# Tokens behind the first experts only normalised, their scale and bias moved to the column pieces and to GpSimd, and TensorE's overflow branch placed ahead of the ending

## The reference

```python
mod = silu(c) @ ada_w[i] + ada_b[i]
sh1, sc1, g1, sh2, sc2, g2 = split(mod, 6)
h = x * (1 + sc1) + sh1
y = mixer_i(h)                               # neighbourhood, then grouped-query
x = layer_norm(alpha * x + (1 + g1) * y, ln_g[i, 0], ln_b[i, 0])
h = x * (1 + sc2) + sh2
y = hierarchical_moe(h)                      # 32 experts, 2 per token
x = layer_norm(alpha * x + (1 + g2) * y, ln_g[i, 1], ln_b[i, 1])

def layer_norm(x, g, b):
    mu, var = x.mean(-1), square(x - mu).mean(-1)
    return (x - mu) * rsqrt(var + 1e-5) * g + b
```

## Time and profile before

| | |
|---|---|
| median of three runs | 1537.4 us (1534.27 to 1539.09) |
| the profiled execution's own time | 1536.41 us |
| its span, from first to last instruction | 1534.6 us |
| mean granted TensorE clock | 0.957 of full speed |
| busy: PE, DVE, ACT, POOL | 1365.2, 547.1, 213.0, 85.5 us |
| read from HBM | 530.27 MB |

### The profile page before, as it was taken

The page is one execution under the profiler, slowest core; times in us unless marked ns, Lnnn a source line. Parts: engine busy times, 40 slices in busy tenths (PEclk is TensorE's granted clock), DMA queues, the critical chain, the costliest instruction groups (busy, mean ns, idle before and its releaser), DMA issues.

```text
span 1534.6 us, 28498 instructions
## 1 busy us (share of the span) xinstructions
PE 1365.2 (89%) x12850; PEld 869.8 (57%) x12850; DVE 547.1 (36%) x1251; ACT 213.0 (14%) x570; POOL 85.5 (6%) x91
## 2 busy tenths in 40 slices
PE   7999999999999998879879787888999798798794
PEld 4886488578886655436436343467655364354451
DVE  3596659665843221111111105584211111111113
ACT  2230123022332000000000002442100000000000
POOL 3100111000003000000000001100200000000000
PEclk9999999999999999989889899999999998998998
DMA  9657945878869999999999997338999999999995
GB/s 345 224 195 260 334 170 201 284 269 300 316 269 397 413 427 427 426 426 427 427 427 425 428 398 276 110 112 339 398 416 427 426 427 426 427 426 427 426 421 200
DMA packets 95001, 533.31 MB, mean 348 GB/s; under 512 B 5121, under 2 KB 7361, under 8 KB 71057
## 3 DMA queue, kind: packets, MB, share of 16 engines
q1 hardware_dynamic: 91264, 519.40, 83.8%
q0 software_dynamic: 3600, 11.94, 2.2%
HBM read 530.27 MB, written 1.05 MB: 346 GB/s over the span
## 4 chain that ended last, share of the span: by engine, by line
PE 61%; DMA 29%; DVE 7%; ACT 1%; issue 1%; DVEq 0%; SPq 0%; ACTq 0%
PE bk L453 26%; PE bk L913 16%; DMA AR<-in_moe_w_down 14%; DMA ring<-in_moe_w_down 14%; PE bk L945 8%; PE bk L976 4%; DVE mpart L1061 3%; PE bk L449 2%; PE bk L672 1%; ACT AR L1890 1%; DVE AR L1053 1%; PE bk L687 1%; PE bk L643 1%; DMA ring<-in_w_in 1%; DVE sm L1064 1%
## 5 line engine op out<-in xcount | busy, mean ns | idle before, releaser
L913 PE MATMUL bk<-ring,AR 128*32 128x128 f32 x4480 | 268.2, 409 | 1.8 <-DMA ring<-in_moe_w_up 1.8
L913 PE MATMUL bk<-AR 128*32 128x128 f32 x3712 | 223.1, 409 | 4.2 <-DMA AR<-in_moe_w_up 4.1
L1053 DVE TENSOR_TENSOR AR<-bk,AR 128x128 f32<-128x128 f32 (+2 forms) x106 | 41.3, 389 | 515.2 <-ACT AR L1890 449.7
L913 PEld LDWEIGHTS bk<-ring,AR 128*32 128x32 f32 x4480 | 176.7, 127 | 83.8 <-DMA ring<-in_moe_w_up 4.8
L453 PE MATMUL bk<-ring,AR 128*128 128x256 f32 (+2 forms) x736 | 213.5, 448 | 6.7 <-ACT AR L1890 3.4
L1890 ACT ACTIVATE AR<-bk 128x512 f32<-128x512 f32 (+4 forms) x174 | 70.4, 427 | 921.3 <-PE bk L913 757.3
L913 PEld LDWEIGHTS bk<-AR 128*32 128x32 f32 x3712 | 145.3, 127 | 74.1 <-DMA AR<-in_moe_w_up 7.1
L453 PEld LDWEIGHTS bk<-ring,AR 128*128 128x128 f32 x736 | 140.5, 194 | 71.8 <-issue 55.0
L945 PE MATMUL bk<-ring,AR 128*32 128x512 f32 x544 | 139.2, 711 | 43.9 <-DMA ring<-in_moe_w_down 43.9
L453 PE MATMUL bk<-AR,ring 128*128 128x256 f32 (+1 forms) x832 | 170.6, 364 | 1.6 <-DVE diag L1053 1.6
L453 PEld LDWEIGHTS bk<-AR,ring 128*128 128x128 f32 x832 | 147.4, 190 | 21.4 <-issue 3.5
(11 more groups left out here) (159 smaller groups left out, 876.6 us busy)
## 6 DMA issues: line engine op xcount, KB each, us to landing
ring<-in_moe_w_gate SPq DMA_DIRECT2D x36, 2048.0 KB, 29.0
ring<-in_moe_w_up SPq DMA_DIRECT2D x34, 2048.0 KB, 26.6
AR<-in_moe_w_up SPq DMA_DIRECT2D x30, 2048.0 KB, 29.9
ring<-in_moe_w_down SPq DMA_DIRECT2D x30, 2048.0 KB, 34.4
AR<-in_moe_w_gate SPq DMA_DIRECT2D x28, 2048.0 KB, 26.9
AR<-in_moe_w_down SPq DMA_DIRECT2D x26, 2048.0 KB, 34.3
ring<-in_ada_w SPq DMA_DIRECT2D x24, 2048.0 KB, 10.5
ring<-in_w_in SPq DMA_DIRECT2D x12, 2048.0 KB, 14.7
```

What stands on the lines that cost most here:

```text
L913: ins = eng.matmul(o[32 * f:32 * f + 32, 128 * m:128 * m + 128], XG[u][:, c, 32 * j:32 * j + 32], w[:, c, f::4], start=c == 0, stop=c == N ...
L1053: return eng.tensor_tensor(o, a, b, op)
```

## The change

Behind the first experts VectorE only subtracts the mean and multiplies by the deviation, one tensor_scalar for each tile, and tells "xn" at once. The gain and bias of that layer norm are combined with `mod` (`norm_columns(1, 1, 0, "comb1", 1)`, three small VectorE instructions in the first quarter of the first experts) and are applied when the transposed columns are written: ScalarE writes columns 0 to 3 of each tile, VectorE columns 4 to 7. For the residual GpSimd multiplies `X` by `ln_g` and adds `ln_b`, four tensor_tensor of 128x1024 behind its last rsqrt of the grouped-query layer; the two rows go to `RES`, in the arena, by loads behind "xn" in place of those of `norm_after(0)`. `out_quarter` waits for "res", and SyncE waits for it ahead of all weights of the second experts. The gate rows are made behind "r00". TensorE's test for overflow stands ahead of `down_rows` in both layers, with the ending in both arms.

```diff
+        RES = view(6912, D), view(7936, D)
@@ TensorE, grouped()
-                common(1, "g")
                 for t in range(NT):
                     norm_cols(1, t)
                 for f in ("k0", "k1", "q00", "K0", "K1", "q10", "r00"):
                     unit(f)
+                common(1, "g")
@@ TensorE, experts(i), last quarter
+                    def ending():
                         o = down_rows()
                         down_end(o, 0)
                         combine(0)
                         down_end(o, 1)
+                        combine(1)
+                    pe.wait_ge(sem("cnt"), i + 1)
+                    kept = pe.n, dict(pe.past), pe.last, list(n_results)
+                    with eng.If(eng.value_load(cnt[0:1, NE:NE + 1]) > CAP):
+                        ending()
+                        overflow(i)
+                    pe.n, pe.past, pe.last, n_results[:] = kept
+                    with eng.Else():
+                        ending()
@@ TensorE, behind experts(i)
-                pe.wait_ge(sem("cnt"), i + 1)
-                with eng.If(eng.value_load(cnt[0:1, NE:NE + 1]) > CAP):
-                    overflow(i)
@@ VectorE
-            def last_cols():
-                v.wait_ge(*filled("nT", 1, 1, 1))
+            def odd_cols(t):
+                v.wait_ge(*filled("nT", 1, t, 1))
                 for a in range(4):
                     c = 4 + a
-                    ins = ts(HT[:, c, 128:256], bank("nT", 1, 1, 1)[:, 128 * a:128 * a + 128],
-                             mod[:, 1, 8 + c:9 + c], ALU.mult, mod[:, 1, c:c + 1], ALU.add)
+                    ins = ts(HT[:, c, 128 * t:128 * t + 128], bank("nT", 1, t, 1)[:, 128 * a:128 * a + 128],
+                             COMB[:, 1, 0, c:c + 1], ALU.mult, COMB[:, 1, 1, c:c + 1], ALU.add)
@@ VectorE, out_quarter
+                if i:
+                    v.wait_ge(sem("res"), t + 1)
@@ VectorE, grouped()
-                last_cols()
+                odd_cols(0)
+                odd_cols(1)
@@ VectorE, experts(i), q == 0
+                            if not i:
+                                norm_columns(1, 1, 0, "comb1", 1)
@@ VectorE, last_norm(i)
+                if not i:
+                    for t in range(NT):
+                        v.wait_ge(sem("lrs"), n_dev[0] - 1 + t)
+                        v.tell(ts(X[:, t, :], X[:, t, :], bn_a[:, t, 0:1], ALU.subtract, st2[:, t:t + 1], ALU.mult), sem("xn"), 3 + t)
+                    return
@@ ScalarE, early_cols(t)
-                s.wait_ge(sem("mod"), 8)
-                for h in range(1 if t else 2):
+                s.wait_ge(sem("comb1"), 1)
+                s.wait_ge(*filled("nT", 1, t, 0))
+                for c in range(4):
+                    ins = act(HT[:, c, 128 * t:128 * t + 128], bank("nT", 1, t, 0)[:, 128 * c:128 * c + 128], ACT.Identity,
+                              bias=COMB[:, 1, 1, c:c + 1], scale=COMB[:, 1, 0, c:c + 1])
@@ ScalarE, grouped()
-                gate_rows(1, "g1", GB_)
                 for f in ("k0", "k1", "q00", "K0", "K1", "q10", "r00"):
                     take(f)
+                gate_rows(1, "g1", GB_)
@@ GpSimd
-            norm_after(0)
+            g.wait_ge(sem("xn"), 4)
+            for n, name in enumerate(("ln_g", "ln_b")):
+                small(RES[n], A[name][0, 1:2, :].to_broadcast([P, D]), "row1")
             for n, f in enumerate(ROPED):
                 ...
+            g.wait_ge(sem("row1"), 32)
+            for t in range(NT):
+                for h in range(2):
+                    g.wait_ge(*filled("nT", 1, t, h))
+                g.step(tt(X[:, t, :], X[:, t, :], RES[0], ALU.mult))
+                g.chain()
+                g.tell(tt(X[:, t, :], X[:, t, :], RES[1], ALU.add), sem("res"), t + 1)
@@ SyncE, ahead of the weights of experts(i)
+                if i:
+                    sp.wait_ge(sem("res"), 2)
```

More of the change, by code:

```diff
@@ L977, in combine @@
                                            start=True, stop=True), "cb", i, q, n, t)
-                    if q == NQ - 1:
+                    if q < NQ - 1:
+                        down(0)
+                        down(1)
+                        combine(0)
+                        combine(1)
+                        continue
+                    def ending():
                         o = down_rows()
@@ L1440, in deviation, with norm_columns @@
                 v.tell(ts(st[:, 28 + t:29 + t], bn_a[:, t, 1:2], LN_EPS, ALU.add), sem("lvar"), n_dev[0])
-            def last_cols():
-                v.wait_ge(*filled("nT", 1, 1, 1))
+            def odd_cols(t):
+                v.wait_ge(*filled("nT", 1, t, 1))
                 for a in range(4):
                     c = 4 + a
-                    ins = ts(HT[:, c, 128:256], bank("nT", 1, 1, 1)[:, 128 * a:128 * a + 128],
-                             mod[:, 1, 8 + c:9 + c], ALU.mult, mod[:, 1, c:c + 1], ALU.add)
+                    ins = ts(HT[:, c, 128 * t:128 * t + 128], bank("nT", 1, t, 1)[:, 128 * a:128 * a + 128],
+                             COMB[:, 1, 0, c:c + 1], ALU.mult, COMB[:, 1, 1, c:c + 1], ALU.add)
                     if a == 3:
-                        free(ins, "nT", 1, 1, 1)
+                        free(ins, "nT", 1, t, 1)
                     else:
                         v.step(ins)
-            def norm_columns(n, i, k):
+            def norm_columns(n, i, k, told, value):
                 sc, sh = mod[:, i, 8 * (k + 1):8 * (k + 1) + 8], mod[:, i, 8 * k:8 * k + 8]
@@ L1459, in norm_columns @@
                 v.chain()
-                v.tell(tt(COMB[:, n, 1], COMB[:, n, 1], sh, ALU.add), sem("comb"), i + 1)
+                v.tell(tt(COMB[:, n, 1], COMB[:, n, 1], sh, ALU.add), sem(told), value)
             def router_weights(i):
@@ L1533, in side @@
                     elif kind == "n":
-                        norm_columns(2 * i, i, 3)
+                        norm_columns(2 * i, i, 3, "comb", i + 1)
                     elif kind == "o":
@@ L1565, in neighbourhood @@
                 extract(6)
-                norm_columns(0, 0, 3)
+                norm_columns(0, 0, 3, "comb", 1)
                 gate_rows(0)
@@ L1869, in last_norm @@
                     ins = stt(X[:, t, :], X[:, t, :], st2[:, t:t + 1], LN_OUT[1], ALU.mult, ALU.add)
[L1870 to L1873, removed]
+                    v.tell(ins, sem("xl"), t + 1)
             for l in range(DEPTH):
@@ L2043, in early_cols @@
             def early_cols(t):
-                s.wait_ge(sem("mod"), 8)
-                for h in range(1 if t else 2):
[L2046 to L2054, removed]
+                s.wait_ge(sem("comb1"), 1)
[3 more added lines that the diff above has]
+                              bias=COMB[:, 1, 1, c:c + 1], scale=COMB[:, 1, 0, c:c + 1])
+                    if c == 3:
+                        free(ins, "nT", 1, t, 0)
+                    else:
+                        s.step(ins)
             def raw_cols(i, t):
```

## The result

The changed kernel is slower by 0.3%, at the edge of what can be told from no change: median of eight runs 1541.9 us (1537.47 to 1544.32) against 1537.3 us of eight of the kernel before (1534.27 to 1539.4), a ratio of 1.0029 [1.0017, 1.0040]. The profiled execution took 1537.47 us, the fastest of its eight, with a span of 1535.7; its granted clock was 0.954.

A forecast was written before the change was run, and what follows sets the result against it. It took the experts as bound by DMA and the grouped-query layer by its own chain, mostly VectorE. Terms -2.9 - 3.2 + 0.4 + 8.4 - 0.7 = +2.0 us on the median 1537.4 gave 1539.4 us, range 1531 to 1544.

The forecast's parts named there:

- The loads: First experts without the gain and bias loads: gate and up pieces end 1.3 us sooner, last down pieces land 2.7 sooner.
- The branch in the first experts: TensorE's overflow test ahead of the down rows costs 4.94 us, partly hidden; the stretch to the end piece gives -2.9 us.
- Rival (c): The branch costs more than 4.94 us ahead of the down rows: 1544.7 us if 8, 1549 if 10; chance 0.15.
- Statistics to "k0": Grouped-query layer's start: one tensor_scalar per tile, columns split over two engines, nothing in front of the transposes; -3.2 us.
- The gate rows: Behind "r00", their 1.85 us partly fill TensorE's 1.49 us wait for ScalarE; +0.4 us.
- GpSimd's four: Residual products and sums in the grouped-query layer each hold one two-input VectorE instruction about 2.1 us; +8.4 us.
- The end: Second experts with the branch ahead of the down rows: end piece done at 1515.6 us against 1516.3; -0.7 us.

The follow-up runs named there:

- g5: g1 with the two 0.52 MB gain and bias rows loaded again at their old places in the first experts, unread; 1536.5 us, ratio 0.9991.
- h2: g1 measured again, beside h3; 1533.6 us, ratio 0.9967 to the kernel before.
- e3: The changed kernel with only TensorE's overflow test put back behind the last combine; 1540.2 us, ratio 1.0020 to the kernel before.
- g1: The changed kernel with the residual on VectorE and TensorE's overflow test back behind the last combine (e2 and e3 together); 1534.4 us, ratio 0.9975.
- g3: g1 with a second, short test and branch ahead of the down rows that jumps over one instruction; 1533.1 us, ratio 0.9969.
- e2: The changed kernel with the residual's four products and sums moved from GpSimd to VectorE; 1532.1 us, ratio 0.9964 to the kernel before.
- h3: e2 measured again, beside h2; 1533.0 us, ratio 0.9972 to the kernel before.
- g2: e2 with the gate rows back in front of the transposes; 1532.0 us, ratio 0.9955 to the kernel before.

## Why the prediction was right and where it was not

The time lay in the range and the change within 0.3%, for the most part for the reasons given. By its steps:

1. **The loads**: right. -1.3 to the last hidden transpose was forecast; it is -1.2 and -1.1. The two profiles with these loads have 427.8 and 427.9 us there (before, g5), ten of the eleven without them 426.2 to 427.1, and one, h2, 428.3. The last down pieces' 2.7 us show in g5 as 2.6 from the start to the first combine.
2. **The branch in the first experts**: this is the term that was mis-sized. The step says "the branch costs 4.94, taken from the gap", and draws the first row at 907.6 - 902.7 behind the transpose. It takes 6.4 to 6.6 us in all fourteen places where it stands ahead, in both expert stages of seven profiles. What was wrong is that the price was read from the gap. "Same code, same full DMA queue" held: the jump itself takes 6.05 to 6.38 us ahead of the down rows and 6.15 to 6.30 behind the first experts' last combine (before, e3, g1, h2, g3, g5). But the gap of 4.94 leaves out the 1.43 us that ran under the last combine's matmuls. The prediction took the 4.94 as all that the profile shows of the branch; asked for the branch's own line, it has a record of 6.20 us, and from that some 6.4 could have been forecast. The first row itself took the 3.5 us forecast (3.64), the two behind it 4.46 in place of 3.8. From the first experts' start to the first combine both profiles of the changed kernel are 0.8 us better than before (442.7 against 443.6), not 2.9. Rival (c) had the direction, but its break-even of 7.9 us wasn't reached: against before the stretch still gains a little. That gain is the loads', not the branch's: with the loads gone and the branch behind, the first combine comes 1.5 to 2.1 us sooner still (e3, g1, h2).
3. **Statistics to "k0"**: right. VectorE's tensor_scalar takes 0.81 us (0.8 estimated; two in 1.69), and 10.98 us became 7.43 and 7.42: -3.6 where -3.2 was forecast. Of that some 0.9 comes from the branch's leaving: with it behind, the same distance is 8.3 to 8.4 us (g1, h2, g3, g5, e3). The other 2.6 are the 1.85 us of gate rows, which no longer stand between, and the 1.38 that TensorE waited for ScalarE, less what its transposes take longer (3.5 to 3.7 us against 2.88).
4. **The gate rows**: +0.4 forecast. "k0" to the first scores is 31.4 us in the changed kernel, +0.9, but 30.4 and 30.5 in e2 and h3 with the same order. So between 0 and +0.4, and the rest is the clock: the 48 matmuls from "k0" on take 21.83 us at a granted clock of 0.95 in the changed kernel, against 20.84 at 1.00 before and in e2.
5. **GpSimd's four**: right, in mechanism, place and size. +8.4 forecast; VectorE's three groups grew by 8.3, TensorE's wait by 8.31 (11.12 - 2.81), e2 took 8.7 off the median, and TensorE's way from the first scores to the second experts is 112.2 to 115.1 us in the three profiles that have them there, and 104.9 to 108.0 in the eight that don't (before, e2, h3, g1, h2, g2, g3, g5). In that long stretch part of it is the granted clock, 0.92 or 0.90 in those three and 0.89 to 0.95 in the eight: beside e2, also at 0.92, the first profile's 112.2 is 5.5 us more and not 6.6. By the exclusion that the Trainium skill states (SBUF — State Buffer, "Who interferes with whom") the full length of 9.6 us would be lost; the trace has 2.0 to 2.1 us lost by each of GpSimd's, which took 2.55 us in the mean, since the held instruction's own 0.4 to 0.75 us are no loss. So a held instruction lasts 2.45 to 2.82 us, and the rule describes it well. For rsqrt the prediction looked at VectorE alone. VectorE was indeed not held: its tensor_scalar of 128x1024 ran in 0.81 us beside the second rsqrt, as long as the one behind it. But GpSimd's own instruction grew, from 0.56 us to 0.91 in all twelve profiles with the tensor_scalar, and to 1.41 beside the scalar_tensor_tensor of 1.28 us in the kernel before. That fits GpSimd as the one that waited; which of the two gives way, no run here varies. SyncE's wait for "res" moved the first load of the second experts to 1001.61 us, as soon as GpSimd was through, at no cost that the last stage shows (461.0 against 461.2).
6. **The end**: missed by the same term as step 2. -0.7 was forecast; from the last hidden transpose to the last stage's first combine it is 15.7 us and, again, 16.3, against 15.6: +0.1 and +0.7. With 6.5 us for the branch the step's own working gives +0.3: the rows then end at 1515.5, behind the 1514.5 at which the end piece lands, so 1.0 of the 1.6 counts.

With 6.5 us for the branch step 2 is 1.6 us dearer and step 6 1.0, and the sum is +2.0 + 2.6 = +4.6 in place of +2.0; the two measurements have +4.6 and +3.2. That the first agrees to the tenth is luck, since the two measurements differ by 1.4 us.

What the change contains is worth keeping: with the residual on VectorE it is 0.28 to 0.45% faster than the kernel before (e2, h3, g2), and so faster than both kernels.

## What to carry to other kernels

Work moved to an idle engine is free only if what it touches is free too: look at what the busy engine is doing at that moment, not at its own share. A wide elementwise instruction on GpSimd held one of VectorE's two-input ones for nearly its whole length, while the same work on VectorE took half as long and fitted a gap. And see which side grew: beside tiny rsqrt it was GpSimd's instruction and not VectorE's. Price a jump by its own record and not by the gap that it leaves: a gap is what remains when the work that the engine still had in hand is over, and at another place less may be in hand. A test whose jump is short costs almost nothing (0.24 us).

## What was unexpected of the hardware

The far jump of TensorE took 6.05 to 6.38 us in twenty places (fourteen ahead of the down rows, six behind the first experts' last combine), with the DMA engines full each time (share 1.01 to 1.05), and 3.36 to 3.62 us behind the second experts' last combine, where they are idle (share 0.02, six places). Windows over the jump alone, of the changed kernel and then of the kernel before, with the columns of the earlier trace rows:

```profile
901.24:907.38 6.14, 0.00 (x0) 0.00 (x0) 0.05 (x1) 0.00 (x0) 0.00 (x0) 0.59 1.02 388
```

```profile
924.85:931.05 6.20, 1.43 (x4) 0.36 (x2) 5.28 (x10) 0.00 (x0) 1.95 (x2) 1.00 1.04 385
1522.11:1525.65 3.54, 1.60 (x4) 0.38 (x2) 2.57 (x4) 0.00 (x0) 0.00 (x0) 1.00 0.02 5
```

The DMA queues of the changed kernel from 901 to 907.5 us, and in e3 from 923.6 to 929 us (packets, MB, share):

```profile
q1 hardware_dynamic: 849, 2.45, 98.4%
q14 instruction: 4, 0.03, 1.4%
q8 instruction: 1, 0.02, 1.1%
```

```profile
q1 hardware_dynamic: 1033, 2.08, 103.8%
q8 instruction: 1, 0.02, 1.3%
```

The weights' packets are larger in the first (2.9 KB in the mean against 2.0), and packets of q14 lie in it (the same queue has five from 901 to 908 us in g1, whose TensorE doesn't jump there, so they are hardly TensorE's own). Neither matters to the jump, which takes 6.15 us in the first and 6.22 in the second. That it takes 2.7 us less where only its own packet moves fits a fetch that waits behind the weights' packets. But place and code differ there too and no run varies the load alone, so this cause is not shown.
